# Sample attention by four sequences and four heads, with keys turned by VectorE in 32x32 blocks

## The chip, the cores and the metric

The kernel runs on one core of one Trainium2 chip. The metric is the device time of one execution in microseconds; "before" stands at 1657.56 us, the median of 3 runs (1657.11 to 1657.65).

## The reference

One step of a decoder layer (1024 channels, 8 heads of 64) for 1024 prompt tokens and, with the same weights, 8 sample sequences of 8 new tokens each. A sample sequence attends to its 1024 past keys and values, which lie in a paged cache (8 pages of 128 tokens, found by a page table), and to its own new ones. The attention is a stick-breaking one:

```python
z = q @ k.T / sqrt(64) + bias_h
log_beta = log_sigmoid(z)
log_stay = where(causal, log_beta - z, 0)
log_after = reverse_cumsum(log_stay) - log_stay
o = where(causal, exp(log_beta + log_after), 0) @ v
```

Around it stand RMSNorm, one input projection (conv gates, q, k, v, and 2 x 1024 gate channels), a gated short convolution, two output projections merged by the sigmoids of the gates, W_out, and a squared-ReLU MLP of 4096 channels. Everything is float32.

## The kernel before

The program is written engine by engine. A list `order`, built by hand, holds the steps of the first part, and PE, ACT, DVE and SP each walk it and issue their share of each step. Dense products split both sides into a high and a low part and run as three matmuls (L1126). SP issues nearly all DMAs, in the order of that list: a command that has to wait holds up all behind it.

The prompt's attention runs first, beside the projections of q, k, v and the convolution. Then comes the step `p1_end`, and then the **sample attention**, laid between the halves of the gate projection. There are 96 gate halves, each of 12 matmuls of up to 364 columns; the dictionary `beside` says which sample steps follow which half. Four iterations j (`NITER`) do the whole:

- An iteration takes two sequences and all eight heads. 16 pages of keys, in 4 groups g of 4 pages, go into the tiles `cache[g]`. `page_group` (L861, L863) issues a group on SP: 4 loads of a page number into a register, then 4 DMAs of a whole page, 128 tokens x 512 channels.
- `page`: PE turns a page in four 128x128 transposes (L1320). ACT (even pages, L1651) and DVE (odd ones, L1945) copy the result from PSUM into `kct`.
- `s_logits` (L1332), one per group: four matmuls of 32 rows x 512 keys, one per pair of heads, side by side in the four column quarters of the array. The weights are `qblk`, in which `own_q` has put each head's queries on its own half of the partitions, zeros elsewhere.
- `s_new` (L1339): the logits of the new keys. `s_cap` (L1951, L1953): bias and cap. `s_softplus`, `s_suffix` (a reverse scan, L1968), `s_weights`: the stick-breaking weights, 128 rows of 1088. `s_turn_w` (L1349) turns them.
- `sums` (L1364), one per group of value pages: 16 matmuls of 32 x 128, then `s_new_sum` (L1372) for the new values after each second group. `s_out` (L1379): PE turns the sums `so`, DVE copies each head's part to `br`.

The value groups use the same four tiles as the key groups. SP therefore loads a value group when the keys that lay there have been turned, and a key group when the sums have read the values: its number loads wait for PE's semaphores `s_turned` and `sums_done`. Between them SP issues a gate weight tile (L824, two DMAs) and a store of gates (L870) every six halves. After the last `s_out` the output projections start.

```python
for t in range(4 * GRAN):
    h = starts[j] + (t // 2 if j == 0 else t)
    beside[h].append(("page", j, t))
    if t % GRAN == GRAN - 1:
        if j == 0: beside[h].append(("load", "k", 1, t // GRAN))
        else: beside[h].append(("load", "v", j - 1, t // GRAN))
```

Of the kernel before, what the change touches and what calls it, by code (L numbers as in the profile page):

```python
# [38 lines left out]
P = 128  # L39
# [7 lines left out]
N_IDENT, N_EARLY, N_STEPS = 2, 5, 78  # L47
# [3 lines left out]
def ds(start, size):  # L51
    return bass.ds(start, size)


def hybrid_layer(nc, x_prompt, x_sample, cache_k, cache_v, state_conv, page_table, norm1_w, w_in, conv_w,
# [16 lines left out]
    NITER = NSEQ // 2  # L72
    assert PAGE == P and 2 * HD == P and DC == NPAIR * P and NB == 8 and PAST == 8 * P and 2 * NEW * NSEQ == P
# [24 lines left out]
    with ctx:  # L98
# [14 lines left out]
        ones = place("ones", [P, P], F32)  # L113
        diag_cap = place("diag_cap", [P, P], F32)
        new_cap = place("new_cap", [P, NITER * SMP], F32)
        bias_p = place("bias_p", [P, NH], F32)
        bias_s = place("bias_s", [P, 1], F32)
# [94 lines left out]
        TILE = 4 * NEW  # L212
        qblk = place("qblk", [P, 2 * NPAIR * TILE], F32)
# [85 lines left out]
        kct_act, kct_dve = sem("kct_act"), sem("kct_dve")  # L299
# [247 lines left out]
        for j in range(NITER):  # L547
# [10 lines left out]
            for g, after in enumerate((9, 10, 11, 12) if last else (10, 12, 16, 19)):  # L558
                beside[at + after].append(("sums", j, g))
                if g % 2:  # L560
                    beside[at + after].append(("s_new_sum", j, g // 2))
# [17 lines left out]
        S_TURNS = [e for e in order if e[0] in ("page", "s_turn_w", "s_new", "s_out")]  # L579
# [49 lines left out]
        def by_dve(t):  # L629

            return t % 2 == 1

        def kct_copied(eng, j, t):

            if by_dve(t):
                eng.wait_ge(kct_dve, j * (2 * GRAN) + (t + 1) // 2)
            else:
                eng.wait_ge(kct_act, j * (2 * GRAN) + t // 2 + 1)
# [178 lines left out]
        def _(sp_):  # L817
# [82 lines left out]
            for e in order:  # L900
# [16 lines left out]
                elif e[0] == "p1_end":  # L917
                    with nc.allow_non_contiguous_dma(reason="small constants"):
                        for n in range(P // NEW):
                            sp_.dma_start(bias_s[n * NEW:(n + 1) * NEW, :],  # L920
                                          att_bias[:, n // 4 * 2 + n % 2:n // 4 * 2 + n % 2 + 1].to_broadcast([NEW, 1])).then_inc(bias_in, 16)
# [7 lines left out]
                elif e[0] == "load":  # L929
                    _, what, j, g = e  # L930
                    if what == "k":
                        if j == 1:
                            sp_.wait_ge(s_turned, s_no["page", 0, GRAN * g + GRAN - 1] + 1)
                        elif j >= 2:
                            sp_.wait_ge(sums_done, (j - 2) * GRAN + g + 1)
                        page_group(j, g, ck, key_use(j))
                    else:
                        if j < NITER - 1:
                            sp_.wait_ge(s_turned, s_no["page", j + 1, GRAN * g + GRAN - 1] + 1)
# [57 lines left out]
        def _(pool):  # L997
# [49 lines left out]
            for m in range(P // NEW):  # L1047
                n = m // 2 % 2
                cap = cap_of(n) if m in (0, 2) else cap_of(2)
# [5 lines left out]
                if m not in (0, 2):  # L1055
                    step(g.tensor_tensor(cap_of(n), cap_of(n), cap, ALU.mult))
            step(g.tensor_scalar(ones[:, 0:2 * NEW], ones[:, 0:2 * NEW], MASKED, Z_MAX, ALU.mult, ALU.add))
            step(g.memset(new_cap[:, :], MASKED))
            for j in range(NITER):
                for n in range(2):  # L1060
                    at = j * SMP + (2 * j + n) * NEW
# [55 lines left out]
        def _(pe):  # L1117
# [58 lines left out]
            def s_turn_bank(e):  # L1176

                n = s_no[e]
                if n >= 2:
                    was = S_TURNS[n - 2]  # L1180
                    if was[0] == "page":
                        kct_copied(pe, was[1], was[2])
                    elif was[0] == "s_turn_w":
# [6 lines left out]

            def own_queries(n, p):

# [945 lines left out]
```

## Time and profile before

| | |
|---|---|
| time, median of 3 runs | 1657.56 us |
| profiled execution | 1656.68 us, span 1654.7 us |
| mean granted TensorE clock | 0.999 |
| sample attention | 448 to 683 us, between gate halves |
| busy share of the span | PE 99%, DVE 42%, ACT 31%, POOL 34% |
| DMA | 157.55 MB, mean 95 GB/s |

The span runs from the first to the last instruction of the profiled execution; its time also has what lies around the span. Busy time counts an engine as working also where its instructions overlap. SP issues DMAs and loads registers, and has no busy row: its queue is read from the timeline, from the view of one source line, and from the view of waits.

### The profile page before, as it was taken

The numbers are of one execution on the slowest core, as the hardware profiler recorded it, in microseconds if no ns is written. First come the engines' busy times: TensorE is split into PE (matmuls) and PEld (weight loads), VectorE is DVE, ScalarE is ACT, GpSimd is POOL, SyncE is SP. The second block draws the span as 40 slices with busy tenths as digits, with TensorE's granted clock in tenths as the row PEclk, the third lists the DMA queues.
The fourth block names the chain that finished last, engine by engine and source line by source line (L and its number), as shares of the span: only waits on it lengthen the run. The fifth ranks groups of instructions, "written<-read, shape, count | busy, mean of one in ns | idle before, by whom it ended". The sixth has DMA issues, their size and how long they took to land.

```text
span 1654.7 us, 24985 instructions
## 1 busy us (share of the span) xinstructions
PE 1644.6 (99%) x9956; PEld 1520.6 (92%) x9956; DVE 694.0 (42%) x1156; ACT 516.9 (31%) x1001; POOL 569.2 (34%) x402
## 2 busy tenths in 40 slices
PE   9999999999999999999999999999999999999998
PEld 8999999999988889999889998899888998899987
DVE  7785868859421222466334330032211331022333
ACT  7565655656322222422245220022100220012111
POOL 5212212112212111232884334733347324652510
PEclk9999999999999999999999999999999999999999
DMA  5202112021276677442552111321113111221211
GB/s 161 66 26 68 39 39 73 21 63 42 96 241 196 208 230 228 164 143 91 172 178 77 52 52 64 102 65 50 53 64 115 49 42 64 89 83 46 89 51 57
DMA packets 145006, 157.55 MB, mean 95 GB/s; under 512 B 9119, under 2 KB 99899, under 8 KB 144892
## 3 DMA queue, kind: packets, MB, share of 16 engines
q1 hardware_dynamic: 144746, 155.93, 29.7%
q8 instruction: 79, 1.29, 0.3%
q14 instruction: 35, 0.29, 0.1%
q10 hardware_dynamic: 146, 0.04, 0.0%
HBM read 136.96 MB, written 18.98 MB: 94 GB/s over the span
## 4 chain that ended last, share of the span: by engine, by line
PE 89%; DVE 6%; ACT 3%; issue 1%; POOL 0%; DVEq 0%; ACTq 0%; POOLq 0%
PE ps L1126 51%; PE ps L1418 10%; PE ps L1423 10%; PE ps L1421 9%; DVE sp L1901 2%; PE ps L1320 2%; DVE zc L1893 1%; PE ps L1276 1%; PE ps L1286 1%; PE ps L1364 1%; PE ps L1332 1%; ACT sp L1604 1%; PE ps L1303 1%; PE ps L1302 1%; DVE br L1849 1%
## 5 line engine op out<-in xcount | busy, mean ns | idle before, releaser
L1126 PE MATMUL ps<-xh,wh 128*128 128x364 f32 (+1 forms) x956 | 323.7, 339 | 0.7 <-DVE xl L1874 0.6
L1126 PE MATMUL ps<-xh,wl 128*128 128x364 f32 (+1 forms) x956 | 313.8, 328 | 0.0
L1126 PE MATMUL ps<-xl,wh 128*128 128x364 f32 (+1 forms) x956 | 313.8, 328 | 0.0
L1113 POOL TENSOR_TENSOR wl<-raw,wh 128x1024 fp32r<-128x1024 f32 x106 | 256.3, 2418 | 19.1 <-POOL wh L1110 18.9
L1126 PE MATMUL ps<-yh,wh 128*128 128x384 f32 (+1 forms) x768 | 250.5, 326 | 0.2 <-DVE yl L2070 0.2
L1126 PE MATMUL ps<-yh,wl 128*128 128x384 f32 (+1 forms) x768 | 250.5, 326 | 0.0
L1110 POOL CAST wh<-raw 128x1024 fp32r<-128x1024 f32 x106 | 111.1, 1048 | 404.8 <-issue 383.1
L1126 PE MATMUL ps<-yl,wh 128*128 128x384 f32 (+1 forms) x768 | 250.3, 326 | 0.0
L1728 ACT ACTIVATE ts<-tt 128x384 f32<-128x384 f32 (+1 forms) x96 | 48.8, 508 | 553.8 <-DVE tt L2082 553.7
L1027 POOL CAST wh<-raw 128x1024 fp32r<-128x1024 f32 x48 | 50.8, 1059 | 479.1 <-issue 205.3
L1126 PEld LDWEIGHTS ps<-xh,wh 128*128 128x128 f32 x956 | 179.7, 188 | 17.0 <-issue 15.3
L2018 DVE TENSOR_TENSOR x<-ps,x 128x512 f32<-128x512 f32 x90 | 60.0, 690 | 320.5 <-PE ps L1423 302.2
L1126 PEld LDWEIGHTS ps<-xl,wh 128*128 128x128 f32 x956 | 180.1, 188 | 0.7
L1126 PEld LDWEIGHTS ps<-xh,wl 128*128 128x128 f32 x956 | 179.7, 188 | 0.0
L1418 PE MATMUL ps<-wh,hh 128*128 128x512 f32 x468 | 179.0, 390 | 0.6 <-POOL wl L1113 0.6
L1423 PE MATMUL ps<-wl,hh 128*128 128x512 f32 x468 | 163.4, 389 | 0.0
L1421 PE MATMUL ps<-wh,hl 128*128 128x512 f32 x416 | 161.9, 389 | 0.0
L1036 POOL TENSOR_TENSOR wl<-raw,wh 128x1024 fp32r<-128x1024 f32 x48 | 116.6, 2428 | 97.2 <-DVE zc L1903 91.4
L2082 DVE TENSOR_SCALAR tt<-ps 128x384 f32<-128x384 f32 (+1 forms) x96 | 51.4, 535 | 233.0 <-PE ps L1126 231.6
L1126 PEld LDWEIGHTS ps<-yh,wh 128*128 128x128 f32 x768 | 144.1, 188 | 1.0 <-issue 0.4
L1126 PEld LDWEIGHTS ps<-yl,wh 128*128 128x128 f32 x768 | 144.1, 188 | 0.0
L1126 PEld LDWEIGHTS ps<-yh,wl 128*128 128x128 f32 x768 | 144.1, 188 | 0.0
(190 smaller groups left out, 2632.2 us busy)
## 6 DMA issues: line engine op xcount, KB each, us to landing
raw<-in_w_down SPq DMA_DIRECT2D x112, 256.0 KB, 2.9
raw<-in_w_in SPq DMA_DIRECT2D x80, 256.0 KB, 3.5
cache<-in_cache_k SPq DMA_DIRECT2D x64, 256.0 KB, 3.6
cache<-in_cache_v SPq DMA_DIRECT2D x64, 256.0 KB, 3.7
raw<-in_w_up SPq DMA_DIRECT2D x64, 256.0 KB, 3.2
raw<-in_w_out SPq DMA_DIRECT2D x48, 256.0 KB, 2.9
gates<-gst SPq DMA_DIRECT2D x16, 544.0 KB, 6.0
gb<-gates SPq DMA_DIRECT2D x16, 544.0 KB, 5.7
```

Source lines behind the costliest of these rows:

```text
L1027: g.tensor_copy(wh[s][:, :], raw[s][:, :]).then_inc(w_hi, 1)
L1036: g.tensor_tensor(wl[s][:, :], raw[s][:, :], f32(wh[s][:, :]), ALU.subtract).then_inc(w_split, 1)
L1110: g.tensor_copy(high[:, :], raw[n % 3][:, :]).then_inc(w_hi, 1)
L1113: g.tensor_tensor(low[:, :], raw[n % 3][:, :], f32(high[:, :]), ALU.subtract).then_inc(w_split, 1)
L1126: ins = mm(out, lhs[:, k * P:(k + 1) * P], rhs[:, x], start=(first and a == 0 and m == 0), stop=(last and a == n - 1 and m == 2))
L1320: ins = tr(bank(tb, p * P, (p + 1) * P), cache[g][:, (a * NPAIR + p) * P:(a * NPAIR + p + 1) * P], ident[:, :])
L1418: mm(out, hi, w, start=k == 0, stop=False)
L1421: mm(out, low[:, k * SEQ + b * P:k * SEQ + b * P + P], w, start=False, stop=False)
L1423: return mm(out, hi, lo_w, start=False, stop=last)
L1728: A(ts_[m % 2][:, 0:z - a], tt[:, 0:z - a], ACT.Square).then_inc(s_made, 1)
L2018: V_.tensor_tensor(x, step_bank(step_no[g, b, h]), x, ALU.add).then_inc(step_free, 1)
L2082: V_.tensor_scalar(tt[:, 0:z - a], step_bank(t, 0, z - a), 0.0, None, ALU.max).then_inc(step_free, 1)
```

## The change

The sample attention is cut another way. An iteration takes **four sequences and four heads** in place of two and eight. Each sequence's keys lie in their own 32 partitions.

- **Loads.** `key_group(j, g)` brings pages 2g and 2g+1 of each of the four sequences, half of the channels: 8 number loads and 8 DMAs of 32 partitions x 4 pieces x 256 channels. `value_group(j, g)` brings the 8 pages of sequence g, half of the channels: 8 number loads and 8 DMAs of 128 x 256. The order of the groups and the buffers stay. The number loads now wait for `kct_made` (DVE) where they waited for `s_turned`.
- **Turning.** PE's page transposes and the copies of ACT and DVE are gone. DVE transposes 128x512 of a key tile in 32x32 blocks, 4 such instructions per group, straight from `cache` to `kct`.
- **Logits.** A head has two 32-channel halves in the 32 partitions of each sequence; `qblk` holds the four sequences' queries on the four quarters. Per group 8 matmuls of 32 x 256 keys in place of 4 of 32 x 512. The new keys use a second tile `qpad`, with 4 matmuls in place of 8.
- **Sums.** Per sequence 8 pages x 4 heads and the new values x 4 heads: 36 matmuls of 32 x 64 in place of 16 of 32 x 128 and, every second group, 4 of 32 x 128.
- **Small things.** `own_q` copies 16 pieces (and 2 for `qpad` in every second iteration) in place of 4; `s_out` 4 in place of 2; the bias comes in 8 small DMAs in place of 16; two GpSimd steps on constants fall away.

```diff
-            def page_group(j, g, src, use):
-
-                numbers = [sp_.value_load(pages[0:1, ds(j * (2 * N_PAGES) + g * GRAN + n, 1)]) for n in range(GRAN)]
-                for n, page in enumerate(numbers):
-                    sp_.dma_start(cache[g][:, n * NPAIR * P:(n + 1) * NPAIR * P].rearrange("p (o n) -> p o n", o=1),
-                                  src[ds(page, 1), :, :].rearrange("o p n -> p o n")).then_inc(page_in[g], 16)
+            def key_group(j, g):
+
+
+                b, c = j // 2, j % 2 * (HALF)
+                for q in range(2):
+                    numbers = [sp_.value_load(pages[0:1, ds((4 * b + a) * N_PAGES + 2 * g + q, 1)]) for a in range(4)]
+                    for a, page in enumerate(numbers):
+                        sp_.dma_start(cache[g][a * 32:a * 32 + 32, q * 2 * 512:(q + 1) * 2 * 512].rearrange("p (k c) -> p k c", k=4),
+                                      ck[ds(page, 1), :, c:c + HALF].rearrange("o (k p) c -> p (o k) c", p=32)).then_inc(page_in[g], 16)
+
+            def value_group(j, g):
+
+
+                b, c = j // 2, j % 2 * (HALF)
+                for q in range(2):
+                    numbers = [sp_.value_load(pages[0:1, ds((4 * b + g) * N_PAGES + 4 * q + a, 1)]) for a in range(4)]
+                    for a, page in enumerate(numbers):
+                        at = (4 * q + a) * (HALF)
+                        sp_.dma_start(cache[g][:, at:at + HALF].rearrange("p (o n) -> p o n", o=1),
+                                      cv[ds(page, 1), :, c:c + HALF].rearrange("o p n -> p o n")).then_inc(page_in[g], 16)
...
-                        page_group(j, g, ck, key_use(j))
+                        key_group(j, g)
...
-                        page_group(j, g, cv, value_use(j))
+                        value_group(j, g)
...
-                elif e[0] == "page":
-                    _, j, t = e
-                    g, a = t // GRAN, t % GRAN
-                    if a == 0:
-                        pe.wait_ge(page_in[g], key_use(j) * 64 + 64)
-                    tb = s_turn_bank(e)
-                    for p in range(NPAIR):
-                        ins = tr(bank(tb, p * P, (p + 1) * P), cache[g][:, (a * NPAIR + p) * P:(a * NPAIR + p + 1) * P], ident[:, :])
-                    ins.then_inc(s_turned, 1)
                 elif e[0] == "s_logits":
...
-                    n, half = g // 2, g % 2
-                    kct_copied(pe, j, GRAN * g + GRAN - 2)
                     kct_copied(pe, j, GRAN * g + GRAN - 1)
                     if g == 0:
                         if j:
                             pe.wait_ge(s_zc, j)
-                        pe.wait_ge(qblk_made, j * 4 + 4)
-                    for p in range(NPAIR):
-                        ins = mm(ps[p * TILE:(p + 1) * TILE, (ZB + half) * 512:(ZB + half + 1) * 512], own_queries(n, p),
-                                 kct[g % 2][:, p * 512:(p + 1) * 512], start=(n == 0), stop=(n == 1))
+                        pe.wait_ge(qblk_made, (j + 1) * 16)
+                    keys = kct[g % 2][:, :].rearrange("p (m c x) -> p c m x", m=8, c=8)
+                    at = ZB * 512 + g * 2 * P
+                    for f in range(2):
+                        for h in range(4):
+                            own = (h * 2 + f) * TILE
+                            ins = mm(ps[h * TILE:(h + 1) * TILE, at:at + 2 * P], qblk[:, own:own + TILE], keys[:, h * 2 + f, :, :],
+                                     start=(f == 0), stop=(f == 1))
                     ins.then_inc(logits_done, 1)
...
-                    if half == 0 and n == 0 and j == 0:
+                    if g == 0 and j == 0:
                         pe.wait_ge(end_rows_made, 1)
-                    pe.wait_ge(page_in[g], value_use(j) * 64 + 64)
-                    for a in range(GRAN):
-                        for p in range(NPAIR):
-                            at = (half * GRAN + a) * P + p * TILE
-                            ins = mm(ps[p * TILE:(p + 1) * TILE, SUM[n] * 512:SUM[n] * 512 + P], swT[:, at:at + TILE],
-                                     cache[g][:, (a * NPAIR + p) * P:(a * NPAIR + p + 1) * P], start=(half == 0 and a == 0), stop=False)
+                    pe.wait_ge(page_in[g], value_use(j) * 128 + 128)
+                    to = SUM[n] * 512 + g % 2 * HD
+                    for t in range(N_PAGES):
+                        for h in range(4):
+                            at, c = t * P + h * TILE, t * 4 * HD + h * HD
+                            ins = mm(ps[h * TILE:(h + 1) * TILE, to:to + HD], swT[:, at:at + TILE], cache[g][:, c:c + HD],
+                                     start=(t == 0), stop=False)
                     ins.then_inc(sums_done, 1)
-                elif e[0] == "s_new_sum":
-                    _, j, n = e
-                    pe.wait_ge(swt_made, j * 3 + 3)
-                    for p in range(NPAIR):
-                        at = N_PAGES * P + p * TILE
-                        ins = mm(ps[p * TILE:(p + 1) * TILE, SUM[n] * 512:SUM[n] * 512 + P], swT[0:SMP, at:at + TILE], vs[:, p * P:(p + 1) * P],
+                    for h in range(4):
+                        at, c = N_PAGES * P + h * TILE, (j % 2 * 4 + h) * HD
+                        ins = mm(ps[h * TILE:(h + 1) * TILE, to:to + HD], swT[0:SMP, at:at + TILE], vs[:, c:c + HD],
                                  start=False, stop=True)
-                    ins.then_inc(so_full, 1)
...
-                elif e[0] == "page":
-                    _, j, t = e
-                    if not by_dve(t):
-                        kct_free(act, j, t)
-                        act.wait_ge(s_turned, s_no[e] + 1)
-                        A(blocks(kct[t // GRAN % 2][:, :], 512)[:, :, t % GRAN * P:(t % GRAN + 1) * P],
-                          blocks(bank(TURN + s_no[e] % 2)), ACT.Copy).then_inc(kct_act, 1)
...
+                b, c = j // 2, j % 2 * 2
+                for h in range(2):
+                    for f in range(2):
+                        r = slice(h * HD + f * 32, h * HD + f * 32 + 32)
+                        for a in range(4):
+                            dst = qblk[a * 32:a * 32 + 32, :].rearrange("p (w h f x) -> p w h f x", w=2, h=2, f=2)[:, :, h, f, a * NEW:(a + 1) * NEW]
+                            src = blocks(qs[r, :], SMP)[:, c:c + 2, (4 * b + a) * NEW:(4 * b + a + 1) * NEW]
+                            V_.tensor_copy(dst, src).then_inc(qblk_made, 1)
...
-                    if by_dve(t):
-                        kct_free(v, j, t)
-                        v.wait_ge(s_turned, s_no[e] + 1)
-                        V_.tensor_copy(blocks(kct[t // GRAN % 2][:, :], 512)[:, :, t % GRAN * P:(t % GRAN + 1) * P],
-                                       blocks(bank(TURN + s_no[e] % 2))).then_inc(kct_dve, 1)
+                    g, a = t // GRAN, t % GRAN
+                    if j == 0 and t == 0:
+                        v.wait_ge(ends_turned, 1)
+                    kct_free(v, j, t)
+                    if a == 0:
+                        v.wait_ge(page_in[g], key_use(j) * 128 + 128)
+                    V_.transpose(kct[g % 2][:, a * 512:(a + 1) * 512], cache[g][:, a * 512:(a + 1) * 512]).then_inc(kct_made, 1)
```

What stands on each engine's queue. First SP, at the first group of values (tile 139 is `cache[0]`). Before, from the number loads to the gate store:

```order
L861 TENSOR_LOAD pages x4
L863 ISA
L863 DMA cache_139<-in_cache_v 128x512
L863 ISA
L863 DMA cache_139<-in_cache_v 128x512
L863 ISA
L863 DMA cache_139<-in_cache_v 128x512
L863 ISA
L863 DMA cache_139<-in_cache_v 128x512
L824 DMA raw_60<-in_w_in 128x4x128 x2
L870 DMA gates<-gst_80 128x1088
```

Now, up to the middle of the same group (four more DMAs follow, then the same weight loads and gate store):

```order
L870 TENSOR_LOAD pages x4
L873 ISA
L873 DMA cache_139<-in_cache_v 128x256
L873 ISA
L873 DMA cache_139<-in_cache_v 128x256
L873 ISA
L873 DMA cache_139<-in_cache_v 128x256
L873 ISA
L873 DMA cache_139<-in_cache_v 128x256
L870 TENSOR_LOAD pages x4
L873 ISA
L873 DMA cache_139<-in_cache_v 128x256
```

Eight number loads and eight DMAs of half the size stand where four and four stood; `raw` and `gates` come behind twice as many commands. Next DVE, around the cap of an iteration (`s_cap` writes `zs_c`, `own_q` writes `qblk`, `kct` are the turned keys). Before:

```order
L1970 TENSOR_TENSOR zs_c<-zs_c,sp_s 128x1088
L1945 COPY kct_144<-ps 128x4x128
L1945 COPY kct_145<-ps 128x4x128 x2
L1945 COPY kct_144<-ps 128x4x128 x2
L1945 COPY kct_145<-ps 128x4x128 x2
L1979 COPY br<-ps 64x4x8 x2
L1951 SCALAR_TENSOR_TENSOR zs_c<-ps,bias_s,new_cap 128x64
L1953 TENSOR_SCALAR zs_c<-ps,bias_s 128x1024
L1860 COPY qblk<-qs 64x4x8 x4
```

Now, a little behind the cap of the second iteration:

```order
L1854 COPY qblk<-qs 32x2x8 x16
L1858 COPY qpad<-qs 64x4x32 x2
L1949 STREAM_TRANSPOSE kct_145<-cache_139 128x512 x2
L1971 SCALAR_TENSOR_TENSOR sp_s<-sp_s 128x1088
L1973 TENSOR_TENSOR zs_c<-zs_c,sp_s 128x1088
L1949 STREAM_TRANSPOSE kct_145<-cache_139 128x512
L1949 STREAM_TRANSPOSE kct_146<-cache_140 128x512 x2
L1984 COPY br<-ps 64x2x8 x4
L1949 STREAM_TRANSPOSE kct_146<-cache_140 128x512 x2
L1949 STREAM_TRANSPOSE kct_145<-cache_141 128x512 x4
```

The copies from PSUM, which wait for a PE transpose, have given way to transposes that read `cache`, and there are twice as many of them; the scan (128x1088) stands between them as before.

## Rows read from the trace of the kernel before

**Rows 1.** The page, part 1: busy time, share of the span, instructions.

```profile
span 1654.7 us, 24985 instructions
PE 1644.6 (99%) x9956; PEld 1520.6 (92%) x9956; DVE 694.0 (42%) x1156; ACT 516.9 (31%) x1001; POOL 569.2 (34%) x402
```

**Rows 2.** Timeline of PE, 456 to 684 us: start, us, engine, line, operation.

```profile
456.55 1.03 PE L1320 MATMUL ps<-ident,cache 128*128 128x128 f32 x8
459.42 1.04 PE L1320 MATMUL ps<-ident,cache 128*128 128x128 f32 x8
...
488.77 0.43 PE L1339 MATMUL ps<-ks,qblk 128*32 128x64 f32 x16
...
550.97 0.60 PE L1320 MATMUL ps<-ident,cache 128*128 128x128 f32 x4
553.41 0.60 PE L1320 MATMUL ps<-ident,cache 128*128 128x128 f32 x4
...
554.05 1.07 PE L1332 MATMUL ps<-kct,qblk 128*32 128x512 f32 x8
...
649.00 1.08 PE L1364 MATMUL ps<-cache,swT 128*32 128x128 f32 x32
650.01 0.42 PE L1372 MATMUL ps<-vs,swT 64*32 64x128 f32 x8
...
683.07 0.27 PE L1379 MATMUL ps<-ident,so 128*128 128x128 f32 x1
```

**Rows 3.** Windows of the sample attention: busy (count) per engine, clock, DMA share, GB/s.

```profile
448.00:683.00 235.00, 235.00 (x2032) 209.40 (x2031) 53.53 (x77) 61.37 (x111) 48.15 (x28) 1.00 0.65 210
460.00:480.00 20.00, 20.00 (x145) 17.67 (x145) 4.15 (x6) 4.99 (x10) 3.42 (x2) 1.00 0.91 301
```

**Rows 4.** The chain that ended last, 440 to 700 us: shares, and one piece.

```profile
by line: PE ps L1126 73.4%; PE ps L1320 10.8%; PE ps L1364 6.2%; PE ps L1332 6.1%; PE ps L1349 1.5%; PE ps L1372 1.1%; PE ps L1339 0.4%; PE ps L1379 0.3%; PE ps L1303 0.1%; PE ps L1302 0.1%; PE ps L1286 0.0%; PE ps L1310 0.0%
...
448.73 7.98 PE ps L1126 x48
```

**Rows 5.** Waits of SP's queue, 446 to 642.6 us: total, times, longest.

```profile
SPq L861 <- PE ps L1320: 31.9, 6, 11.8
SPq L861 <- PE ps L1364: 29.0, 5, 6.8
SPq L861 <- PE ps L1379: 10.0, 3, 3.8
```

**Rows 6.** Groups by form, 448 to 684 us: busy, mean ns, idle before.

```profile
L1945 DVE COPY kct<-ps 128x512 f32<-128x512 f32 x32 | 22.1, 691 | 129.0 <-PE ps L1320 104.5 <-PE ps L1379 24.4
L1651 ACT ACTIVATE kct<-ps 128x512 f32<-128x512 f32 x32 | 19.1, 598 | 107.9 <-PE ps L1320 107.9
L1968 DVE TENSOR_TENSOR_SCAN sp_s<-sp_s 128x1088 f32<-128x1088 f32 x4 | 11.6, 2908 | 3.6 <-ACT sp_s L1671 3.6
```

**Rows 7.** SP's lines, 446 to 642.6 us: ns min/median/max, first and last start.

```profile
L861 SPq TENSOR_LOAD <-pages x120: 260/268/1648, 446.4 to 639.3; - x120
L863 SPq DMA_DIRECT2D cache<-in_cache_k x64: 332/333/1307, 448.0 to 602.1; - x64
L863 SPq DMA_DIRECT2D cache<-in_cache_v x56: 332/333/1297, 498.0 to 642.3; - x56
DMA to landing us min/median/max: 2.6/3.7/6.0
L824 SPq DMA_DIRECT2D raw<-in_w_in x22: 389/447/510, 460.2 to 633.7; - x22
L870 SPq DMA_DIRECT2D gates<-gst x11: 360/431/1442, 461.3 to 634.3; - x11
L920 SPq DMA_DIRECT2D bias_s<-in_att_bias x16: 295/296/1312, 437.9 to 444.3; - x16
```

**Rows 8.** Timeline of SP, 446 to 530 us.

```profile
447.97 12.10 SPq L863 DMA_DIRECT2D cache<-in_cache_k  x16
460.19 0.94 SPq L824 DMA_DIRECT2D raw<-in_w_in  x2
...
523.78 1.93 SPq L863 DMA_DIRECT2D cache<-in_cache_v  x4
527.12 1.89 SPq L863 DMA_DIRECT2D cache<-in_cache_k  x4
```

More of the change, by code:

```diff
@@ L560, in hybrid_layer @@
                 if g % 2:
-                    beside[at + after].append(("s_new_sum", j, g // 2))
+                    beside[at + after].append(("s_copy", j, g // 2))
                 if j == NITER - 2:
@@ L578, in hybrid_layer @@
         assert not beside
-        S_TURNS = [e for e in order if e[0] in ("page", "s_turn_w", "s_new", "s_out")]
+        S_TURNS = [e for e in order if e[0] in ("s_turn_w", "s_new", "s_out")]
         s_no = {e: n for n, e in enumerate(S_TURNS)}
@@ L1054, in _ @@
                                      pattern=[[0, NEW]], channel_multiplier=-1))
-                if m not in (0, 2):
+                if m >= 4:
                     step(g.tensor_tensor(cap_of(n), cap_of(n), cap, ALU.mult))
-            step(g.tensor_scalar(ones[:, 0:2 * NEW], ones[:, 0:2 * NEW], MASKED, Z_MAX, ALU.mult, ALU.add))
+            step(g.tensor_scalar(ones[:, 0:4 * NEW], ones[:, 0:4 * NEW], MASKED, Z_MAX, ALU.mult, ALU.add))
             step(g.memset(new_cap[:, :], MASKED))
-            for j in range(NITER):
-                for n in range(2):
-                    at = j * SMP + (2 * j + n) * NEW
+            for b in range(2):
+                for n in range(4):
+                    at = b * SMP + (4 * b + n) * NEW
                     step(g.tensor_copy(new_cap[:, at:at + NEW], cap_of(n)))
@@ L1180, in s_turn_bank @@
                     was = S_TURNS[n - 2]
-                    if was[0] == "page":
-                        kct_copied(pe, was[1], was[2])
-                    elif was[0] == "s_turn_w":
+                    if was[0] == "s_turn_w":
                         pe.wait_ge(swt_made, was[1] * 3 + was[2] + 1)
@@ L1352, in _ @@
                     _, j, g = e
-                    n, half = g // 2, g % 2
-                    if n == 0:
-                        pe.wait_ge(swt_made, j * 3 + half + 1)
-                    if half == 0 and j:
+                    n = g // 2
+                    if g == 0:
+                        pe.wait_ge(swt_made, j * 3 + 3)
+                    if g % 2 == 0 and j:
                         pe.wait_ge(so_copied, j * 2 - 1 + n)
-                    if half == 0 and n == 0 and j == 0:
+                    if g == 0 and j == 0:
@@ new lines, in _ @@
+                    for t in range(N_PAGES):
[3 more added lines that the diff above has]
+                                     start=(t == 0), stop=False)
+                    ins.then_inc(sums_done, 1)
+                    for h in range(4):
+                        at, c = N_PAGES * P + h * TILE, (j % 2 * 4 + h) * HD
+                        ins = mm(ps[h * TILE:(h + 1) * TILE, to:to + HD], swT[0:SMP, at:at + TILE], vs[:, c:c + HD],
@@ L1938, in _ @@
                     v.wait_ge(qs_made, NPAIR)
+                    V_.memset(qpad[:, :], 0.0).then_inc(qpad_zero, 1)
+                    v.wait_ge(qpad_zero, 1)
                     own_q(0)
```

81 lines of the change are left out of this document (40 added, 41 removed).

## Prediction

> **What bounds the kernel now.** I began with the page. PE is busy 99% of the span and every other engine under half of it [rows 1], so at first sight a microsecond taken from PE is a microsecond off the time. The stretch that the change touches is the sample attention, which is spread between the halves of the gate projection; it begins after PE's transpose of `ends` and ends with the last transpose of `so` at 683.07 us [rows 2]. In the windows view PE has no idle time there, its granted clock is 1.00 (the 2.4 GHz level) and the DMA engines carry 0.65 of their share [rows 3]. The chain of waits agrees: between 440 and 700 us it runs through PE alone, and 10.8% of it are the page transposes, L1320 [rows 4].
>
> So PE bounds the stretch. But it is fed by SP, which issues all page loads in a fixed order, and SP's time is on no "busy" row. The view of who waited for whom shows SP standing idle before its page-number loads (L861) for 31.9 + 29.0 + 10.0 = 70.9 us between 446.0 and 642.6 us [rows 5]. That idle time is SP's whole reserve, and this change spends it.
>
> **What PE gives up.** Two halves of a gate chunk with nothing between them take 7.98 / 4 = 2.00 us each [rows 4]. With one page between them they start 2.44 us apart (550.97 to 553.41), with two pages 2.87 us (456.55 to 459.42) [rows 2]. Iteration 0 has 8 slots of two pages, the others 48 of one: 8 x 0.87 + 48 x 0.44 = 28.1 us of PE. All of it lies before 649.0 us.
>
> PE's other work hardly moves. The logits have the same columns in twice as many matmuls of 256 (L1332 now: 8 records, 1.07 us [rows 2]). In the sums, 32 records of 128 columns take 1.08 us and the new keys' 8 another 0.42 with a start of their own; there will be 72 records of 64 columns in one run. Sixteen records of 64 columns span 0.43 us [rows 2], four side by side, so a round costs no more than some 0.07 us; 18 rounds are at most 1.3 us. A group of sums then costs between 0.1 us less and 0.3 us more, 16 of them -2 to +5 us. I take 0, because PE will be waiting anyway.
>
> **What DVE and ACT get.** ACT loses 32 copies of 598 ns. DVE loses 32 of 691 ns [rows 6] and gets 64 block transposes of 128x512 from SBUF to SBUF. No row shows one. The copy of the same size, 0.69 us, is nearest; the dearest row per column is the scan, 2.9 us for 1088, which gives 1.4 us for 512. Even at 1.4 a group of four takes 5.5 us, while SP will need 6.9 us to load a group (below), so they hide. `own_q` grows from 4 small copies to 16 or 18, behind `s_cap`, some 5 gate halves before the first logits want them: nothing. The bias loads are 8 instead of 16 ahead of a wait that SP meets anyway: nothing.
>
> **What SP gets.** A group of pages is now 4 page-number loads and 4 DMAs of 256 KB. It becomes 8 and 8, each DMA of 128 KB, for keys and for values. What does a command cost SP? The first four groups stand back to back: the first number load is at 446.4 us [rows 7], the 16 DMAs run from 447.97 for 12.10 us [rows 8], so 13.7 / 4 = 3.42 us a group. A clean group takes 3.30 (from 525.71, the end of the one before, to 529.01 [rows 8]). The price hangs on the command, not on the bytes: 256 KB as 128 rows take 333 ns, a bias load of eight 4-byte rows takes 296 ns, a weight load of 512 rows 447 ns [rows 7]. The key DMA is 32x4x256, again 128 rows, the value DMA 128x256. So halving a DMA saves next to nothing, and half a group will cost what a group costs.
>
> The Trainium skill speaks against this (DMA: Bandwidth & Descriptors, Issuing engines are not separate DMA queues): the time on the sequencer to initiate a DMA "is usually small relative to the DMA itself". By it the doubled commands would be free and the sum would be the first rival's. The rows say otherwise here.
>
> Which group decides? The last wait that can hold PE is for the values of the sums (2, 3), which start at 649.00 us today [rows 2]; behind it stand 34.1 us of PE work (683.07 - 649.0) whose own two load groups will come in time: they follow at once on SP, by some 689 us, and are wanted near 702. Its load is the 30th of 32 groups in SP's order (120 number loads up to 639.3 us [rows 7]). Between the first and the 30th SP also issues 22 weight loads and 11 gate stores: 11 x 0.94 + 11 x 0.43 us, with gaps of 0.12 about 18 us [rows 7, 8]. Cross-check on today: 642.6 - 446.4 - 70.9 of waiting leaves 125.3 us of commands; less 18 is 107.3, or 3.58 us a group, pauses included.
>
> New sum: 60 half-groups x 3.45 + 18 = 225 us. I take 3.45, near the back-to-back row, because one long pause of the 3.58 (a number load of 1648 ns [rows 7]) falls between 460 and 480 us, where the DMA share was 0.91 [rows 3]; spread over twice the commands, the same bytes will not crowd so. The 30th group is then issued by 446.4 + 225 = 671.4, lands 3.7 us later [rows 7] at 675.1, and the sums that start at 649.0 today start 26.1 us later. With no reserve left SP never waits, so PE's 28.1 us all turn into waits for `page_in`; the chain moves from PE to SP. The profiled execution took 1656.7 us (span 1654.7 and 2.0 around it), 0.9 under the median of the runs: 1656.7 + 26.1 = 1682.8, so I say **1683 us**.
>
> **Ends of the range.** Cheapest: the clean group 3.30 with every DMA at the bias load's price, 4 x 0.037 less, is 3.15; 60 x 3.15 + 18 = 207, and the fastest landing of 2.6 us gives 656.0, +7.0: 1664. Dearest: 3.58 for the 28 half-groups of values, and for the 32 of keys 4 x 0.114 more (a DMA with three dimensions at the weight load's 447 ns), 4.04: 100 + 129 + 18 = 247; with 3.7 us of landing 697.5, +48.5: 1705.
>
> **Rivals.** *SP keeps up and PE's saving counts.* This is the other side. Without transposes PE would want the 30th group by 649.0 - 28.1 - 3.7 = 617.2, so half a group may cost (617.2 - 446.4 - 18) / 60 = 2.55 us; then the time is 1656.7 - 28.1 = 1629. From 2.55 to 3.01 us part of the gain is left; at 3.01 the change is worth nothing. For it: PE is busy 99% and SP has 70.9 us of reserve. Against it: thirty groups more at 3.42 need 102.6 us, and no row is under 3.15. All of the gain 6%, part of it 5%.
>
> *SP and something more.* Key DMAs now write to 32 partitions each, four of them in turn, in pieces of 1 KB instead of 2. If landing rises from 3.7 to the slowest 6.0 us [rows 7], the sum grows by 2.3. PE will also stand idle for microseconds, which it never does in this stretch today, so no row tells what its clock does then. If it fell to the 1.2 GHz level, that costs nothing while SP decides, but would double part of the 34 us behind the last wait: 4 us for each 4 us spent there. Together about 1690; with dear key DMAs up to 1705. Chance 17%. The Trainium skill (TensorE: Matmul & The Clock Gate, HAM oscillation) does say that waits for a DMA can drop the clock.
>
> *PE as bound, no change.* SP's cost falls right at 3.01 us a half-group: 2%.
>
> **Chances.** The forecast, SP's queue at 3.15 to 3.58 us, 70%; SP and more 17%; full or part gain 11%; no change 2%. Within 0.2% (3.3 us) counts as the same, about what a measurement of this kernel can tell. Faster 0.10, same 0.03, slower 0.87. Range 1664 to 1705.
>
> **What would show it.** Right: PE busy falls below 99%, by 50 us or so, and its waits stand before the sums and logits, released by page loads. SP has no wait at its number loads between 446 and 670 us; a half-group takes 3.3 to 3.6 us; the last `so` transpose is near 709 us instead of 683. DVE's transposes take 0.6 to 1.4 us and end soon after each landing. Wrong: SP still waits for PE or DVE in the stretch, a 128 KB DMA costs it much under 0.3 us, or PE waits for DVE's `kct`.

## The result: 36 us slower, and the profile after

The changed kernel takes 1693.76 us (median of 4 runs, 1690.43 to 1694.63); the kernel before took 1657.34 (4 runs, 1656.72 to 1657.65). The ratio is 1.0218, 95% interval 1.0205 to 1.0230. I had forecast 1683 in 1664 to 1705: the direction and the mechanism held, the size was 11 us short. The profiled execution took 1694.63 us, its span is 1692.9.

The page of the changed kernel, parts 1, 2 and 6 (busy time; granted clock in 40 slices; DMA issues with KB each and us to landing):

```profile
PE 1635.5 (97%) x10372; PEld 1513.8 (89%) x10372; DVE 726.5 (43%) x1257; ACT 498.9 (29%) x969; POOL 569.3 (34%) x400
...
PEclk9999999999989989899999999999999999999999
...
cache<-in_cache_k SPq DMA_DIRECT2D x128, 128.0 KB, 2.5
cache<-in_cache_v SPq DMA_DIRECT2D x128, 128.0 KB, 2.2
```

Before, PE was busy 1644.6 of 1654.7 us [rows 1], so 10.1 idle; now 57.4 are. That is 47 us more idle time and 9 us less work. Its waits, 446 to 730 us (total, times, longest):

```profile
PE ps L1366 <- DMA cache<-in_cache_v: 35.2, 10, 7.3
PE ps L1136 <- ACT gst L1553: 11.1, 2, 9.1
```

L1366 are the sums: they wait for value pages. And SP, which waited 70.9 us in three lines [rows 5]? Between 446 and 700 us this is all:

```profile
SPq L934 <- DVE br L1929: 0.8, 1, 0.8
SPq L870 <- DVE kct L1949: 0.7, 3, 0.3
```

SP has no reserve left. The chain of waits between 440 and 560 us, which was PE alone before [rows 4], now runs through SP's key DMAs (L862), its number loads (L860) and the value group's two lines:

```profile
by line: SPq L862 29.1%; SPq L860 19.5%; issue 14.9%; SPq L873 8.2%; PE ps L1136 6.8%; SPq L870 6.4%; DMA gates<-gst 3.5%; SPq L820 3.0%; DMA cache<-in_cache_v 1.8%; PE ps L1366 1.6%; DVE kct L1949 1.1%; SPq L880 1.0%; PE ps L1329 0.9%; SPq
```

The prices of SP's commands, by line (ns min/median/max, first and last start), against [rows 7]; a DMA of 128 KB costs what one of 256 KB did:

```profile
L860 SPq TENSOR_LOAD <-pages x128: 261/269/916, 447.5 to 631.0; - x128
L862 SPq DMA_DIRECT2D cache<-in_cache_k x128: 316/317/1597, 449.1 to 633.4; - x128
L873 SPq DMA_DIRECT2D cache<-in_cache_v x128: 332/333/1862, 511.7 to 697.0; - x128
```

The place that decides, PE's timeline from 676 to 690 us and the last `so` transpose:

```profile
684.23 1.94 PE L1366 MATMUL ps<-cache,swT 128*32 128x64 f32 x64 [7.33 <-DMA cache<-in_cache_v]
686.10 0.44 PE L1371 MATMUL ps<-vs,swT 64*32 64x64 f32 x8
686.47 0.67 PE L1136 MATMUL ps<-xh,wh 128*128 128x364 f32 x1
...
721.29 0.27 PE L1379 MATMUL ps<-ident,so 128*128 128x128 f32 x1
```

The sums (2, 3) start at 684.23 instead of 649.00, 35.2 us later, and the last `so` transpose at 721.29 instead of 683.07 [rows 2], 38.2 later; from there on the two executions run at a constant distance, and 38.2 is the difference of the spans.

### The profile page after: what moved, and what is told of

It reads as the page before. It is cut to its first block, busy times and chain, and to the rows that moved or that the text cites. A ratio compares the mean times of both kernels' runs of the same rounds, so it can differ in the third digit from the quotient of the medians.

```text
span 1692.9 us, 26313 instructions
## 1 busy us (share of the span) xinstructions
PE 1635.5 (97%) x10372; PEld 1513.8 (89%) x10372; DVE 726.5 (43%) x1257; ACT 498.9 (29%) x969; POOL 569.3 (34%) x400
## 4 chain that ended last, share of the span: by engine, by line
PE 76%; SPq 9%; DVE 7%; issue 3%; ACT 3%; DMA 1%; POOL 0%; DVEq 0%; ACTq 0%; POOLq 0%
PE ps L1136 43%; PE ps L1418 10%; PE ps L1423 10%; PE ps L1421 9%; SPq L873 2%; SPq L862 2%; DVE sp L1900 2%; SPq L870 2%; SPq L860 2%; DVE zc L1892 1%; PE ps L1280 1%; PE ps L1290 1%; ACT sp L1604 1%; PE ps L1307 1%; PE ps L1306 1%
## 5 line engine op out<-in xcount | busy, mean ns | idle before, releaser
L1136 PE MATMUL ps<-xh,wh 128*128 128x364 f32 (+1 forms) x956 | 327.1, 342 | 11.8 <-ACT gst L1553 11.1
L1136 PE MATMUL ps<-xl,wh 128*128 128x364 f32 (+1 forms) x956 | 318.3, 333 | 0.0
L1136 PE MATMUL ps<-xh,wl 128*128 128x364 f32 (+1 forms) x956 | 318.1, 333 | 0.0
L1136 PEld LDWEIGHTS ps<-xh,wh 128*128 128x128 f32 x956 | 183.5, 192 | 22.0 <-issue 19.1
L1136 PEld LDWEIGHTS ps<-xl,wh 128*128 128x128 f32 x956 | 183.7, 192 | 0.7
L1136 PEld LDWEIGHTS ps<-xh,wl 128*128 128x128 f32 x956 | 183.3, 192 | 0.0
```

The lines of the kernel that those rows point to most:

```text
L1136: ins = mm(out, lhs[:, k * P:(k + 1) * P], rhs[:, x], start=(first and a == 0 and m == 0), stop=(last and a == n - 1 and m == 2))
```

## The experiments

My theory: the time is set by how many commands SP issues before the 30th page group is in, not by bytes, transfers, DVE or PE. Rivals: the new shape of the key DMAs, their landing, or DVE's part. "The 30th group's end" below is the end of SP's last DMA of that group: 642.60 us before, 682.39 after the change.

### Doubling the commands of the kernel before

(In all diffs here `...` stands for code left out.)

```diff
-                numbers = [sp_.value_load(pages[0:1, ds(j * (2 * N_PAGES) + g * GRAN + n, 1)]) for n in range(GRAN)]
-                for n, page in enumerate(numbers):
-                    sp_.dma_start(cache[g][:, n * NPAIR * P:(n + 1) * NPAIR * P]...
+                for q in range(2):
+                    numbers = [... the same four ...]
+                    for n, page in enumerate(numbers):
+                        at = n * NPAIR * P + q * 256
+                        sp_.dma_start(cache[g][:, at:at + 256]..., src[ds(page, 1), :, q * 256:q * 256 + 256]...
```

> The kernel before, with each page loaded by two DMAs of 128x256 (the two halves of the channels) behind number loads of their own: 8 and 8 a group as in the change, the same data, all else as before, PE's page transposes too. Theory (the number of SP's commands sets the time): SP's 30 groups take 235 us as they do after the change, the sums (2, 3) start near 684 us and the time is 1691 us (1685 to 1697), though PE has 28 us more work and DVE no transposes. Rival (the new DMA form on 32 partitions, the block transposes or the batching slow the change): within 3 us of 1657.

Measured: 1691.76 us (1689.17 to 1695.38, 4 runs; before 1656.95; ratio 1.0204, interval 1.0187 to 1.0221). The 30th group ends at 683.01. The kernel before becomes as slow as the change by this edit alone, with all of PE's transposes still in it. PE's waits there (446 to 730 us) have the same releaser:

```profile
PE ps L1366 <- DMA cache<-in_cache_v: 21.6, 6, 7.1
PE ps L1322 <- ACT kct L1653: 3.7, 1, 3.7
```

SP's first number load to the 30th group's end took 236.2 us (446.86 to 683.01), against 234.9 in the change. So the 28 us of transposes are worth nothing while SP decides, and the theory stands. This is the run on which the explanation rests. It halves the size of each DMA along with doubling the commands; the next run holds the size and takes commands away.

### Half of the number loads

```diff
-                    numbers = [sp_.value_load(...) for a in range(4)]
+                    if q == 0:
+                        numbers = [sp_.value_load(...) for a in range(4)]
```

> The change, with the second half of each group using the page numbers of the first half again, so that the wrong pages are loaded there: 4 number loads a group instead of 8, 8 DMAs as in the change. Theory (SP's commands): a number load and its register work cost some 0.30 to 0.39 us, 120 of them lie before the 30th group's end, so 36 to 47 us go: 1647 to 1658 us, and PE's wait before the sums (2, 3) shrinks. Rival (the DMAs' landing, their bytes or DVE decide): unchanged, within 3 us of 1694.

Measured: 1654.53 us (1652.90 to 1656.54, 10 runs); the ratio to before is 0.9986 (0.9977 to 0.9996). The 30th group ends at 643.16. Both moved by the same 39.2 us. Of these 1.1 us are an earlier start (446.34 against 447.48, before the stretch that was edited); the other 38.1, for 120 loads, are 0.32 us each, though the load's own row is 0.269. What makes up the rest was not taken apart. No DMA, byte or transpose was taken away, so neither the smaller DMAs nor their shorter rows hold the pages back.

### The key DMAs in the shape of the value DMAs

```diff
-                        sp_.dma_start(cache[g][a * 32:a * 32 + 32, q * 2 * 512:(q + 1) * 2 * 512].rearrange("p (k c) -> p k c", k=4), ...
+                        at = (4 * q + a) * (HALF)
+                        sp_.dma_start(cache[g][:, at:at + HALF].rearrange("p (o n) -> p o n", o=1), ...
```

> The change, with the key DMAs in the form of the value DMAs (128 partitions x 256 elements), so that the key tiles hold their data in the wrong places; the number of commands is the same. Theory (SP's count of commands): nothing, within 3 us of 1694, since a key command takes 317 ns and a value command 333 ns; 128 of them at 16 ns more would be 2 us slower. Rival (the writes to 32 partitions crowd the queue or land late): faster by over 5 us.

Measured: 1694.06 us (1692.62 to 1694.18, 4 runs), ratio 1.0220 (1.0203 to 1.0237); the 30th group ends at 682.87. No effect: the writes to 32 partitions are innocent. Their landing was 2.5 us, that of the value-shaped ones 2.2; the three dimensions made the command no dearer (317 against 333 ns), so the dear end of my range, 447 ns, did not come true.

### The value groups on ACT's queue

The first line leaves SP's stream, the others stand in ACT's at the same place of the order; number loads and DMAs become ACT's.

```diff
-                        value_group(j, g)
+                elif e[0] == "load" and e[1] == "v":
+                    ...
+                    value_group(j, g)
```

> The change, with the value groups (their waits, number loads and DMAs) issued by ACT's queue instead of SP's, at the same places of the order; the computation is whole. Theory (one queue's commands are the bound, and PE's saving is real once it is lifted): SP issues 16 groups less by 642 us, so neither queue is late; PE is the bound again and its 28 us come out: 1629 us (1626 to 1640). Rival a (ACT's own work is held up by 7 us of commands per group, so casts or gate evictions come late and PE waits for ACT): 1640 to 1680. Rival b (something other than the issuing queue holds the pages back, the transfers for instance): 1690 or more.

Measured: 1682.90 us (1680.91 to 1684.02, 4 runs), ratio 1.0158 (1.0141 to 1.0175). Faster than the change by 11 us, but not what I wanted; it is rival a, a little over its upper end. PE's waits, 446 to 700 us:

```profile
PE ps L1119 <- ACT gst L1536: 22.6, 7, 8.5
PE ps L1333 <- ACT zs_c L1669: 11.3, 2, 5.9
PE ps L1349 <- DMA cache<-in_cache_v: 3.8, 1, 3.8
```

ACT's timeline around one group, with a cast of a gate chunk (`gst`) that stands behind it:

```profile
537.52 5.65 ACTq L1553 DMA_DIRECT2D cache<-in_cache_v  x8
543.22 0.47 ACT L1536 ACTIVATE gst<-ps 128x360 f32<-128x360 f32 x1 [6.58 <-issue]
```

PE's waits for pages are almost gone, and waits for ACT have come: 8 DMAs and 8 number loads in a row hold the casts up for 6 to 7 us, and PE has only two banks for gate chunks.

### Keeping half of the page numbers in registers

A real version of the second experiment: the same 32 numbers serve four passes (keys and values of two iterations).

```diff
+            def number(at):
+                if at in page_no:
+                    return page_no[at]
+                n = sp_.value_load(pages[0:1, ds(at, 1)])
+                if at // N_PAGES % 4 < 2:
+                    page_no[at] = n
+                return n
```

> The change, with the page numbers of sequences 4b and 4b+1 kept in SP's registers from their first use, so that each of these is loaded once instead of four times; the computation is whole. 96 of the 240 number loads before the 30th group's end go. Theory (SP's commands): the run with half the numbers took 39.2 us less for 120 loads, 0.327 us each; 96 of them are 31 us: 1662 us (1658 to 1667). Rival (the wrong pages of that run, repeated and so perhaps quicker to read, made it faster, not the loads): within 5 us of 1694.

Measured: 1665.51 us (1664.46 to 1666.82, 4 runs), ratio 1.0054 (1.0038 to 1.0071): 28.3 us less than the change, a little under the 31 of the theory. The 30th group ends at 654.86, 27.5 earlier, or 0.29 us for each of 96 loads. That is no clean price: SP started 1.3 us earlier, and it stood waiting for 9.1 us (6.8 for the sums, 2.3 for DVE), against 1.5 in the change. But the gain of the second experiment was not an effect of its repeated pages.

### Half of each value group on ACT, without and with kept numbers

SP's `value_group` runs `for q in range(1)`, ACT's `for q in range(1, 2)`, at the same places of the order.

> The change, with only the second half of each value group (4 number loads, 4 DMAs) issued by ACT's queue and the first by SP's; the computation is whole. Theory (with all value groups on ACT its casts of the gate halves came 6 to 7 us late behind each group, and PE waited 22.6 us for gst; half as much is hidden between two casts): SP's 46 half-groups end 46 x 3.61 + 18 = 184 us after 446.4, so the sums (2, 3) start near 632 us: 1641 us, and up to 1655 with some waits for ACT. Rival (ACT's queue holds PE up whatever the size of the piece): 1670 or more.

> Both of the two before: the second halves of the value groups on ACT's queue, and SP keeps the page numbers of sequences 4b and 4b+1; the computation is whole. Theory: SP needs 163 us instead of 235, less than the 171 at which PE would be the bound; then PE's 28 us come out but for ACT's delays: 1629 to 1645 us, and at least 3 us less than without kept numbers. Rival (ACT holds PE up, not SP): the same as without kept numbers, within 3 us.

Measured: 1654.28 us without (1652.83 to 1655.88, 10 runs; ratio 0.9982, 0.9973 to 0.9992) and 1648.56 with kept numbers (1648.18 to 1650.30, 4 runs; ratio 0.9953, 0.9936 to 0.9970). Both theories were right in direction and optimistic in size: the first is at the upper end that I allowed, the second 3.6 us over its range. The kept numbers gain 5.7 us here, and 28.3 without the loads on ACT: the two edits do not add up, so SP was no longer the whole bound in the first. There PE waited 2.7 us for value pages and 14.2 for `gst`, while SP stood idle for 14.4 us before its number loads, for the sums. What is left of PE's waits in the second, 446 to 700 us:

```profile
PE ps L1147 <- ACT gst L1564: 8.8, 1, 8.8
PE ps L1377 <- DMA cache<-in_cache_v: 4.0, 2, 2.4
PE ps L1361 <- ACT zs_c L1697: 2.4, 1, 2.4
```

This wait was there in the change itself (9.1 us) and in the first of the two (8.9 of the 14.2); with half the number loads it was 4.2. ACT's waits between 462 and 500 us and SP's timeline show from where:

```profile
ACT gst L1564 <- DMA gates<-gst: 23.3, 2, 18.1
```

```profile
448.54 25.48 SPq L873 DMA_DIRECT2D cache<-in_cache_k  x32
474.13 0.95 SPq L820 DMA_DIRECT2D raw<-in_w_in  x2
475.21 0.43 SPq L891 DMA_DIRECT2D gates<-gst  x1
```

A gate store stands on SP behind the 32 key DMAs of iteration 0; ACT may not write that buffer again before it is stored, and PE waits for ACT.

### The value groups on POOL

As with ACT, but in the stream of POOL (GpSimd), each group at its place between the weight splits, with semaphores of their own for the values.

```diff
+                elif e[0] == "load" and e[1] == "v":
+                    ...
+                    value_group(j, n)
```

> The change, with the value groups issued by POOL instead of SP, at the same places of the order, on semaphores of their own; the computation is whole. POOL has the most idle time in this stretch (busy 48 of 274 us). No row shows what a DMA costs POOL. Theory: up to 1 us a command (8 us of DMAs a group, 128 in all) it hides beside the weight splits: PE is the bound, 1629 us (1626 to 1640). Rival: a DMA costs POOL 2 us or more, so that 16 groups need over 256 us and the weight splits come late: 1680 or more.

Measured: 1666.23 us (1663.85 to 1670.36, 4 runs), ratio 1.0052 (1.0035 to 1.0069). Neither figure: a DMA costs POOL 538 ns, inside what I thought would hide, and yet it did not. POOL's waits, 446 to 700 us, and one group on its timeline:

```profile
POOL cache L1096 <- DVE kct L1955: 40.2, 3, 15.6
POOL cache L1096 <- issue: 36.1, 24, 3.2
```

```profile
505.76 2.37 POOL L1096 DMA_DIRECT2D cache<-in_cache_v  x4 [14.11 <-DVE kct L1955]
510.62 2.29 POOL L1096 DMA_DIRECT2D cache<-in_cache_v  x4 [2.50 <-issue]
512.91 1.05 POOL L1021 CAST wh<-raw 128x1024 fp32r<-128x1024 f32 x1
514.15 2.37 POOL L1030 TENSOR_TENSOR wl<-raw,wh 128x1024 fp32r<-128x1024 f32 x1 [0.19 <-POOL wh L1021]
```

POOL's weight splits and its loads stand in one order, each behind the other's waits; PE waited 19.7 us for value pages and 10.0 for `gst` between 446 and 700 us. I did not take these two apart.

### Gate stores on ACT, then one weight load moved up

The base is the version with half the value loads on ACT and kept numbers. SP's own gate stores go; ACT gets these lines:

```diff
                 A(gst[t % 2][:, a:z], bank(d % 2, 0, z - a), ACT.Copy).then_inc(gate_free, 1)
+                if d % 3 == 2:
+                    act.wait_ge(gate_free, d + 1)
+                    apart(act)
+                    act.dma_start(gates[t], gst[t % 2][:, :]).then_inc(gate_out[t % 2], 16)
```

> The kernel with half the value loads on ACT and kept page numbers, and with the gate stores (gates<-gst) issued by ACT right behind its last cast of a tile instead of by SP; the computation is whole. In the profile without this, one store stood on SP behind 32 key DMAs (issued 475.21 us), so ACT's cast into the same buffer waited 18.1 us and PE 8.8 us for gst. Theory (a queue's commands, again): these 8.8 us go, PE's other waits of about 6 us stay: 1640 us (1636 to 1643), 8 to 9 under 1648.6. Rival (the wait only moves on, to the weights queued at the same place or to the first sums): within 3 us of 1648.6.

> The kernel before, with the gate stores issued by ACT in the same way and nothing else. Theory: PE has no idle time in this stretch of the kernel before, so there is nothing to gain, and 16 commands of 0.4 us more on ACT cost nothing: within 2 us of 1657. Rival (the stores on ACT are worth something or cost something by themselves, whatever the loads): over 3 us away from it.

Measured: 1648.14 us (1647.30 to 1650.16, 5 runs; ratio 0.9947, 0.9934 to 0.9961), against 1648.56 without. The rival was right. The same edit in the kernel before gives 1656.64 (1656.21 to 1657.34, 10 runs; before 1657.06; ratio 0.9998, 0.9989 to 1.0008), as expected: nothing. In the first, the wait for `gst` shrank from 8.8 to 1.2 us and a new one came up (PE, 446 to 700 us; POOL, 446 to 500 us):

```profile
PE ps L1138 <- POOL wl L1048: 6.8, 1, 6.8
```

```profile
POOL wh L1039 <- DMA raw<-in_w_in: 33.4, 2, 28.2
```

The next command behind the 32 key DMAs was a weight tile's load. So I moved that one to between the second and the third key group:

```diff
+                    if (what, j, g) == ("k", 0, 2):
+                        in_tile(6 * NPAIR + early + 2)
```

> The kernel before this one (half the value loads and the gate stores on ACT, kept page numbers), with one weight tile's load (raw<-in_w_in) moved on SP from behind the first four key groups to between the second and the third; the computation is whole. In the profile without this, POOL waited 28.2 us for that load and PE 6.8 us for wl at 478.3 us. Theory (the place in SP's queue made that wait): the 6.8 us go, and some 1.5 us at the 1.2 GHz level behind it; the last keys come 1 us later. PE's other waits of 7 us stay: 1640 us (1637 to 1643), 5 to 10 under 1648.1. Rival (the wait moves on once more, to the last kct of iteration 0 or to the next weights): within 3 us of 1648.1.

Measured: 1645.67 us (1644.05 to 1647.03, 5 runs; before 1656.53; ratio 0.9930, 0.9917 to 0.9944). It is 2.5 us under the one without, inside the band that the rival gave (3 us), not the 5 to 10 of the theory. The two were run apart and the ratios' intervals overlap, so that even this gain is not clear of the noise. The traces are clearer: the wait for `wl` is down from 6.8 to 0.5 us, and most of it has moved on to the keys (PE, 446 to 700 us):

```profile
PE ps L1335 <- DVE kct L1977: 6.2, 2, 4.2
PE ps L1372 <- DMA cache<-in_cache_v: 3.4, 2, 2.5
PE ps L1356 <- ACT zs_c L1696: 1.2, 2, 0.8
PE ps L1142 <- POOL wl L1052: 0.5, 1, 0.5
```

This is the fastest version found, with the whole computation in it: 48 us under the change and 11 under the kernel before.

### What the clock cost

```diff
+                    if (j, g) == (2, 3):
+                        for n_ in range(64):
+                            tr(bank(7, 2 * P, 3 * P), ident[:, :], ident[:, :])
```

> The change, with 64 transposes of `ident` into unused columns of a PSUM bank put on PE ahead of its last long wait, the 7.3 us before the sums (2, 3); about 7 us of work that nobody uses. Theory (the clock costs what the 1.2 GHz level shows, 680.0 to 690.3 us in the profile of the change, where the sums took 1.94 instead of 1.10 us): PE's clock stays at the 2.4 GHz level behind that wait, 3 us less: 1691 us (1690 to 1692). Rival (the clock does not fall for that wait, or the padding delays the sums by as much as it saves): within 1 us of 1694, or up to 2 us more.

Measured: 1693.50 us (1691.46 to 1694.91, 5 runs), against 1693.76 for the change; the runs of the two cover each other, so in the time this is no difference: my 3 us did not show, and the figure is the rival's. In the profiled execution most of them can be seen. PE's timeline there:

```profile
676.21 7.15 PE L1363 MATMUL ps<-ident 128*128 128x128 f32 x64
683.29 1.10 PE L1369 MATMUL ps<-cache,swT 128*32 128x64 f32 x64
```

The windows from 680 to 690 us, of the change and of this run (PEclk is the number behind POOL's):

```profile
680.00:690.00 10.00, 5.77 (x84) 5.43 (x85) 0.98 (x1) 0.28 (x1) 3.16 (x1) 0.50 0.51 155
```

```profile
680.00:690.00 10.00, 10.00 (x136) 9.65 (x135) 1.95 (x1) 1.75 (x3) 0.80 (x1) 1.00 0.57 182
```

With PE kept at work the clock stays at the 2.4 GHz level and the same 64 matmuls take 1.10 us; behind the idle 7.3 us of the change it stood at 1.2 GHz and they took 1.94. From the start of the sums to the last `so` transpose it is 37.06 us in the change, 34.40 here (717.69 - 683.29) and 34.07 before. But the padding itself ran over the arrival: SP's last DMA of the 30th group started at 680.00 here and landed 2.0 us later, at 682.0, 1.3 before the padding ended. So of 2.7 us some 1.4 are left, less than the spread of the runs. The cost of the clock is shown in two traces, not in the median.

## Why the prediction was right, and where it was short

**The bound moves from PE to SP: right.** Doubling SP's commands alone reproduces the result (1691.76), halving the number loads takes 39.2 us back, and the shape of the key DMAs does nothing. A command of 317 ns is short beside a landing of 2.5 us, but 480 number loads and DMAs stand in one line before the 30th group is in. The Trainium skill (DMA: Bandwidth & Descriptors, Issuing engines are not separate DMA queues) calls the sequencer's part of a DMA usually small; by the runs here it is the bound, and the measurement decides.

**The 30th group decides: right.** Where SP is the bound, the profiled time follows that group's end: 1012.2 us behind it in the change, 1012.4 with the doubled commands, 1011.4 with half the numbers, 1010.1 with kept ones.

**The size: the term for SP's commands was too small.** The sum said 60 half-groups x 3.45 + 18 = 225 us. The trace has 234.9 (first number load 447.48, last DMA's end 682.39). The 18 was right: the stretches between page groups with weight loads and gate stores are 18.6 us in all. The half-group was 216.3 / 60 = 3.61. I had set 3.45, under the mean of 3.58, because "the same bytes will not crowd so". That step failed; with 3.58 the same sum would have come to 1690 or 1691. The long pauses did not stay what they were with the same bytes: among the number loads and page DMAs up to the 30th group's end, 9 of 240 took over 0.6 us in the kernel before, 7.1 us above an ordinary 0.3 us each, and 20 of 480 in the change, 15.3 us above it. Without the pauses a half-group is (216.3 - 15.3) / 60 = 3.35 us, and a group before was (107.3 - 7.1) / 30 = 3.34: the clean price did not move, and the pauses doubled. What they follow is open. In the run with half the number loads there are 22 of them in 360 commands, 15.2 us above the ordinary, as many as in the change with a third more commands. So they do not go by the number of commands alone. All six traces in which SP issues 240 page DMAs up to that point have 16 to 23 pauses, but with 120 DMAs there is only the kernel before, and no run tells the number of DMAs from the time that the queue is at work.

**The whole difference of the spans**, from the forecast's terms:

| term | us |
|---|---|
| forecast: start of the sums (2, 3) later | 26.1 |
| SP's commands, 234.9 instead of 225 | +9.9 |
| SP's first load at 447.48 instead of 446.4; the offset is older than the changed stretch | +1.1 |
| from SP's last command to the sums 1.84 us instead of 3.7 | -1.9 |
| PE's work from these sums to the last `so` transpose, 37.06 us instead of 34.07 | +3.0 |
| measured, 1692.9 - 1654.7 | 38.2 |

The last row is nearly all the clock, which stood at the 1.2 GHz level from 680.0 to 690.3 us: with PE kept at work the same piece took 34.40 us, so 2.7 are the clock's. It was in the rival "SP and something more", as 4 us for each 4 us of work behind the last wait that falls into the lower level; the 6.0 us from the sums' start to 690.3 hold 3 us of work or so and cost about as much again. Rated there at 17% together with a slow landing, it came true in that half, and the rival's 1690 is nearer to the measured time than my 1683. The landing went the other way: 2.2 us for the value DMAs in the change, 3.7 before. Of the 1.9 us in the table 0.3 are a slip: the view counts the landing from the command's start, and I added it to the command's end.

**The other marks.** DVE's transposes were to take 0.6 to 1.4 us; they take 0.68, and no matmul waited for them in the change:

```profile
L1949 DVE STREAM_TRANSPOSE kct<-cache 128x512 f32<-128x512 f32 x64 | 40.1, 681 | 45.0 <-PE ps L1329 28.9 <-DMA cache<-in_cache_k 15.8
```

SP's waits in the stretch were gone but for 1.5 us, as said. PE's waits for pages stood before the sums alone, none before the logits. The last `so` transpose was to be near 709 us and came at 721.3, by the terms of the table. "PE busy falls by 50 us or so" was badly put: it is the idle time that grew by 47 us, while the busy time fell by 9 only, as part of PE's work ran at the lower clock between its waits (granted clock 0.91 from 448 to 683 us, 1.00 before). I missed one wait, the 9.1 us for `gst`: the prediction counted the gate stores among SP's commands but did not ask who waits for one that stands behind 32 key DMAs. In the change it should cost nothing, since SP decides later and waits for nobody; that is argued, for the gate stores were not moved in the change itself. With loads on ACT and kept numbers it was the largest wait left.

**The rival on the other side** (SP keeps up: 1629 us) put the break-even at 3.01 us a half-group. Half the number loads bring it to (643.16 - 446.3 - 18) / 60 = 2.98, and the time to 0.9986 of before: the break-even fits. The full 28.1 us were never reached. The best version has 11.3 us of waits left in the stretch; the remaining difference to 1629 was not traced.

## What to carry to other kernels

A queue's idle time before its commands is a reserve like any other: before splitting DMAs, multiply commands (number loads and register work included) by the measured price of one and compare with that reserve. Take the mean price with its long pauses, not the clean one: here they doubled with twice the DMAs and the same bytes. When the commands are moved to another queue, look at what stands behind them there; here groups of four between two casts hid on ACT, groups of eight did not, and each wait removed uncovered the next command in the same line.

## What the runs showed of the hardware that I had not expected

- A dynamic DMA of 128 KB costs SP's queue 317 to 333 ns, one of 256 KB 333 ns, whether it writes 32 or 128 partitions; a number load costs 269 ns by its row and some 0.3 us when it is taken away (0.32 with half the loads, 0.29 with kept numbers, where SP also waited).
- The same DMA issued by ACT takes 340 to 348 ns (medians of the runs with half the value groups there), by POOL 538 ns.
- In the change transfers of half the size landed in 2.2 to 2.5 us instead of 3.7, so the tail behind the last command got shorter. Size is not all of it: with half the value loads on ACT, ACT's DMAs of the same 128 KB took 3.7 to 4.2 us (medians of two runs).
- DVE transposes 128x512 fp32 in 32x32 blocks from SBUF to SBUF in 681 ns, against 691 for its plain copy of that size from PSUM.
